# First feed-forward block by seven block products, with the squares of three of four quads on VectorE

## What is computed

```python
def rms_norm(x, w):
    y = xf * lax.rsqrt(jnp.mean(xf * xf, axis=-1, keepdims=True) + RMS_EPS)
    return (y * w)

def squared_relu_mlp(h, w_up, w_down):          # w_up 1024 x 4096, w_down 4096 x 1024
    return jnp.square(jax.nn.relu(h @ w_up)) @ w_down

x = x + y                                        # y: the mixer's output, through dn_out
x = x + squared_relu_mlp(rms_norm(x, norm_mlp), mlp_w_up, mlp_w_down)
```

## Time and profile before

| | before |
|---|---|
| median of 3 runs | 3104.36 us |
| profiled execution, its time | 3103.91 us |
| profiled execution, its span | 3102.1 us |
| mean granted TensorE clock | 0.987 |
| TensorE busy | 2953.6 us (95%), 14715 matmuls |
| VectorE busy | 1820.8 us (59%) |
| ScalarE busy | 1210.9 us (39%) |
| GpSimd busy | 901.7 us (29%) |

### The profile page before, as it was taken

The page is one execution under the profiler, slowest core; times in us unless marked ns, Lnnn a source line. Parts: engine busy times, 40 slices in busy tenths (PEclk is TensorE's granted clock), DMA queues, the critical chain, the costliest instruction groups (busy, mean ns, idle before and its releaser), DMA issues.

```text
span 3102.1 us, 37785 instructions
## 1 busy us (share of the span) xinstructions
PE 2953.6 (95%) x14715; PEld 2445.9 (79%) x14715; DVE 1820.8 (59%) x2359; ACT 1210.9 (39%) x1929; POOL 901.7 (29%) x684
## 2 busy tenths in 40 slices
PE   7899999989999999999998999999989999999997
PEld 6688888878788888888876777888878778887886
DVE  7566566564365544333366886554574866666866
ACT  5555555553311112221334776222332444444222
POOL 5333332221000000000302886331331444443423
PEclk9999999999999999999999999999999999999999
DMA  3111111112143333111210001011023144446953
GB/s 128 41 48 48 48 48 48 42 62 102 41 129 110 111 113 102 48 48 54 93 53 21 11 9 49 28 35 35 21 75 149 40 157 150 148 148 239 371 207 122
DMA packets 96833, 274.00 MB, mean 88 GB/s; under 512 B 9232, under 2 KB 31248, under 8 KB 92176
## 3 DMA queue, kind: packets, MB, share of 16 engines
q1 hardware_dynamic: 96656, 271.58, 25.0%
HBM read 208.43 MB, written 60.36 MB: 87 GB/s over the span
## 4 chain that ended last, share of the span: by engine, by line
PE 81%; DVE 10%; ACT 4%; issue 3%; POOL 1%; DMA 1%; SPq 0%; POOLq 0%; DVEq 0%; ACTq 0%
PE ps L663 25%; PE ps L1756 11%; PE ps L3068 11%; PE ps L3729 9%; PE ps L3096 7%; DVE b L3677 2%; PE ps L2659 2%; PE ps L1060 1%; DVE b L652 1%; PE ps L2466 1%; PE ps L2437 1%; PE ps L2465 1%; PE ps L1067 1%; PE ps L2480 1%; PE ps L90 1%
## 5 line engine op out<-in xcount | busy, mean ns | idle before, releaser
L663 PE MATMUL ps<-b 128*128 128x512 f32 x3912 | 1009.6, 403 | 29.7 <-DVE b L652 14.4
L663 PEld LDWEIGHTS ps<-b 128*128 128x128 f32 x3912 | 711.4, 191 | 159.2 <-issue 20.1
L1756 PE MATMUL ps<-b 128*128 128x512 f32 x1536 | 361.7, 396 | 0.6 <-DVE b L1924 0.6
L1756 PEld LDWEIGHTS ps<-b 128*128 128x128 f32 x1536 | 288.0, 188 | 69.5 <-DVE b L1924 1.0
L3729 PE MATMUL ps<-b 128*128 128x512 f32 (+1 forms) x1464 | 326.1, 377 | 6.3 <-ACT b L3788 5.9
L3729 PEld LDWEIGHTS ps<-b 128*128 128x128 f32 x1464 | 253.8, 191 | 55.6 <-issue 10.6
L644 ACT ACTIVATE b<-b 128x1024 fp32r<-128x1024 f32 x138 | 145.2, 1054 | 319.5 <-PE ps L1756 242.3
L3121 ACT ACTIVATE b<-b 128x512 fp32r<-128x512 f32 x232 | 142.3, 615 | 270.9 <-PE ps L3096 106.3
L652 DVE TENSOR_TENSOR b<-b 128x1024 fp32r<-128x1024 f32 x138 | 174.2, 1264 | 107.6 <-ACT b L644 98.5
L3068 PE MATMUL ps<-b 128*128 128x512 f32 x960 | 225.9, 393 | 6.0 <-DVE b L3371 3.8
L3068 PEld LDWEIGHTS ps<-b 128*128 128x128 f32 x960 | 180.5, 189 | 48.3 <-DVE b L3371 7.7
(11 more groups left out here) (372 smaller groups left out, 5011.4 us busy)
## 6 DMA issues: line engine op xcount, KB each, us to landing
inner<-b SPq DMA_DIRECT2D x77, 512.0 KB, 2.6
b<-inner SPq DMA_DIRECT2D x35, 1024.0 KB, 13.5
b<-in_down SPq DMA_DIRECT2D x52, 512.0 KB, 4.3
b<-in_mod SPq DMA_DIRECT2D x96, 256.0 KB, 2.6
b<-scratch SPq DMA_DIRECT2D x46, 512.0 KB, 4.4
b<-in_gu SPq DMA_DIRECT2D x44, 512.0 KB, 4.1
b<-in_dn_in SPq DMA_DIRECT2D x32, 512.0 KB, 4.9
b<-in_up SPq DMA_DIRECT2D x32, 512.0 KB, 3.7
```

The costliest lines, as they stand in the source:

```text
L663: ins = e.matmul(ps[:, c], w, h[:, k, c], start=first and k == 0 and i == 0, stop=last and k == KT - 1 and i == 2)
L1756: ins = e.matmul(ps[:, c], w, u[:, at[k], c], start=k == 0 and p == 0, stop=k == n - 1 and p == 2)
```

## The change

The first feed-forward block gets the same scheme. In words:

- 16 up blocks of two FF tiles each. Block 0 is plain (96 matmuls); blocks 1 to 15 have 7 steps of 12. Then 16 down blocks with 7 steps of 12 each. The last two up blocks are interleaved.
- The norm's factor is no longer applied to each up tile: since relu and square let a positive factor per token pass as its square, the block's result is scaled once, at the end, by 1/(mean of squares + eps), and added to x1, which was kept in DRAM meanwhile (`dve_square_last`, in the steps of the last down block: per half tile one multiplication with a row in PSUM, then one addition to x1, each waiting for the one before).
- Per up block VectorE joins three quads with a bank and squares them in place, max(u, 0) * u in one operation; the fourth quad ("21"), and all four of block 0, get relu and square as two ScalarE operations. GpSimd makes four sums of weight quads and four of inner quads. Seven pieces per block are split and stored to DRAM; the down blocks load them back (two blocks' pieces at a time, ring of 9).
- The modulation's slots: 12 of its steps now lie beside dn_out, then one every third up step, one every second down step.
- The statistics of the next norm (`act_stat2`, `pool_stat2`) use the rows of the scaled result as buffers, so their first square waits until x1 rows 0 to 3 are done.
- `PIECES7`, the order of pieces, is changed in the second block too.

The core of the diff:

```diff
+BLOCKS1 = tuple(((2 * b, 2 * b + 1),) for b in range(8))
+PIECES7 = (0, 3, 5, 4, 1, 2, 6)
...
+class WideSquare(Wide):
+    def sums(self, s):
+        if s == self.index[self.na, 0] + 13:
+            return self.na - 1
+        if s == self.index[0, 3] + 4:
+            return 0
+        v = self.which(s - 1, "last")
+        return v if v is not None and 0 < v < self.na - 1 else None
+    def beside(self, s):
+        a, b = self.index[self.na - 2, 0], self.index[self.na, 0]
+        return 6 <= s < a and s % 3 == 0 or s >= b and s % 2 == 0
...
+    def dve_square(self, e, w):
...
+        for i in range(KT):
+            if i:
+                self.dve_weights(e, min(jd + i + 3, jd + KT))
+            for _ in range(2 if i >= 2 else 0):
+                next(beside)
+            if 3 <= i < 7:
+                plain(i - 3)
+            if i == KT - 1:
+                for s in range(4):
+                    self.dve_wide_low(e, w, s)
+                for k in range(4, 7):
+                    plain(k)
+            x = self.x1[:, i, :]
+            e.wait_ge(*self.xl[i].at("dn_out"))
+            e.wait_ge(*self.gm.at(jd + i))
+            e.tensor_tensor(x, x, self.psl[i % 3], ALU.add).then_inc(*V.up("add", i))
...
+        for s in range(4, len(w.steps)):
+            v, i = w.steps[s]
...
+                if 3 <= i < 6:
+                    name = ("12", "22", "11")[i - 3]
+                    u = w.quads(v)[name]
+                    e.wait_ge(*P.at("st", v, i))
...
+                    e.tensor_tensor(u, u, self.square_bank(v, (1, 0, 2)[i - 3]), ALU.add).then_inc(*V.up("q" + name, v))
+                    e.wait_ge(*V.last())
+                    e.scalar_tensor_tensor(out=u, in0=u, scalar=0.0, in1=u, op0=ALU.max, op1=ALU.mult).then_inc(*V.up("u" + name, v))
+            else:
+                self.dve_square_add(e, w, v - w.na, i)
+            self.dve_wide_low(e, w, s + 6)
+            piece = w.piece(s)
+            if piece:
...
+                e.wait_ge(*A.at("thi", p, n))
+                e.tensor_tensor(b[:, 512:1024], w.source(p, PIECES7[n]), b[:, 0:512].bitcast(F32),
+                                ALU.subtract).then_inc(*V.up("tlo", p, n))
+            if v == last:
+                for k, f in {0: ((0, 0), (0, 1)), 1: ((1, 0), (1, 1)), 2: ((2, 0), (2, 1)), 3: ((3, 0), (3, 1), (4, 1), (6, 1)),
+                             4: ((5, 1), (7, 1)), 5: ((4, 0), (6, 0)), 6: ((5, 0), (7, 0))}[i]:
+                    self.dve_square_last(e, w, k, f)
+            if w.beside(s):
+                next(beside, None)
...
+        self.dve_weights(e, w.j0 + 2)
+    def dve_square_last(self, e, w, k, f):
...
+        e.wait_ge(*P.at("rw"))
+        e.wait_ge(*V.last())
+        e.tensor_tensor(y, y, self.psl[3][:, c], ALU.mult).then_inc(*V.up("scaled", k, f))
+        e.wait_ge(*self.xl[k].at("x1"))
+        e.wait_ge(*V.last())
+        ins = e.tensor_tensor(x, x, y, ALU.add)
...
+    def act_square(self, e, w):
...
+            if v == last:
+                for k in {2: (0, 1), 3: (2, 3)}.get(i, ()):
+                    e.wait_ge(*V.at("x1", k))
+                    if k == 0:
+                        e.wait_ge(*V.at("x1", 3))
+                        e.wait_ge(*A.at("cw"))
+                    self.act_stat2(e, self.m1, w.sig, k)
...
+        for k in range(4, KT):
+            e.wait_ge(*V.at("x1", k))
+            self.act_stat2(e, self.m1, w.sig, k)
+        self.act_weights(e, w.j0 + 2)
...
+    def pool_square(self, e, w):
...
+        for s in range(4, len(w.steps)):
...
+            self.pool_wide_sums(e, w, s, 1)
+            p = w.sums(s)
+            if p is not None:
+                u, tq = w.quads(p), w.tq
+                if p:
+                    e.wait_ge(*V.at("tlo", p - 1, 6))
...
+                e.tensor_tensor(tq[0], u["12"], u["11"], ALU.subtract).then_inc(*G.up("t", p, 1))
+                e.wait_ge(*G.last())
+                e.tensor_tensor(u["12"], u["22"], u["12"], ALU.subtract).then_inc(*G.up("t", p, 4))
+                e.tensor_tensor(tq[1], u["22"], tq[0], ALU.subtract).then_inc(*G.up("t", p, 2))
+                e.wait_ge(*G.last())
+                e.tensor_tensor(tq[2], u["21"], tq[1], ALU.subtract).then_inc(*G.up("t", p, 6))
...
@@ sp_between
-            e.wait_ge(*self.mm1[2].at("down", last, k))
+            e.wait_ge(*self.mm1[2].at("x1", k))
```

More of the change, by code:

```diff
@@ L348, in __init__ @@
         n = n_ff
-        self.steps = [(v, i) for v in range(2) for i in range(4)] + [(v, i) for v in range(2, n - 2) for i in range(7)]
+        self.steps = [(v, i) for v in range(n - 2) for i in range(self.last(v) + 1)]
         self.steps += [(n - 2, 0)]
@@ L368, in last @@
     def last(self, v):
-        return 3 if v < 2 else 6
+        return 3 if v < self.plain else 6
     def which(self, s, i):
@@ L641, in act_weights @@
             e.wait_ge(*self.wl[j % RAW].at(j))
-            if j >= SPL:
+            after = j - UNIT["win", 4]
+            if 0 <= after < SPL:
+                steps = self.w1.steps
+                e.wait_ge(*self.mm1[0].at("st", *steps[max(s for s in range(len(steps)) if s // 2 % SPL == after)]))
+            elif j >= SPL:
                 e.wait_ge(*self.gm.at(j - SPL))
@@ L1640, in mlp_slots @@
-    def mlp_slots(self, n_ff, ring, gated):
-        slots = []
-        for kind, f, n in mlp_plan(n_ff, ring):
-            if kind == "up":
-                slots.append((1, ("act", f)))
-                if gated:
-                    slots.append((2, ("mul", f)))
-            else:
-                slots += [(2, ("down", f, m)) for m in range(8)]
-        if not gated:
-            slots = [(2, ("relu", event[1])) if event[0] == "act" else (engine, event) for engine, event in slots]
-        return slots
@@ L3546, in pool_program @@
         self.pool_delta(e)
[L3547 to L3553 removed]
+        self.pool_square(e, self.w1)
         self.pool_stat2(e, self.m1, self.mm1)
```

942 lines of the change are left out of this document (502 added, 440 removed).

## The result

The changed kernel took 3160.22 us (median of 4 runs, 3158.26 to 3161.66); the kernel before, beside it, 3103.76 us. The ratio is 1.0182 (95% interval 1.0164 to 1.0199): **slower by 1.8%**, where 3091.5 was forecast and 3124 was the upper end of the range. The profiled execution took 3158.26 us, span 3156.4, mean granted clock 0.970 (0.987 before). TensorE is busy 2899.0 us instead of 2953.6, so most of the matmul time did go (84 us were forecast). VectorE is busy 2154.0 instead of 1820.8, GpSimd 1209.5 instead of 901.7.

What follows compares the result with a forecast made beforehand. It took TensorE's matmuls to bound the kernel before, VectorE the new up blocks. Terms -83.9 -9.9 +1.0 +5.5 +2 +36 -8 +4 +37.7 +3 sum to -12.6 us: from 3103.91 to 3091.3, stated as 3091.5, range 3062 to 3124.

Steps and rivals of the forecast that it cites:

- Matmuls (-83.9): Whole first feed-forward stage: matmul time falls from 707.0 us to 623.1 us, a gain of 83.9 us.
- The end (+37.7): Stage end: waiting for VectorE's x1 and GpSimd's sums, 48.1 us beyond matmuls before the projection, against 10.4: 37.7 more.
- E: End of the last down block's first product; the first projection was forecast at E + 64.7 us.
- The up blocks (22.5 us, measured 25.0): Blocks 2 to 13: VectorE, colliding with GpSimd, sets 22.5 us a block against TensorE's 19.5, adding 36 us in all.
- held by every GpSimd operation: Rival for the up blocks: every GpSimd operation blocks VectorE, 24.9 us a block, 3120 us in all; chance 0.22.
- ceiling of 25.8: Up blocks: VectorE's 16.6 us alone a block, plus all eight GpSimd operations holding it, give 25.8 us.
- the modulation's matmuls would be hidden (-8): Up blocks: while VectorE sets the pace, some 8 us of TensorE's modulation matmuls cost nothing extra.
- The modulation's slots: Beside dn_out: VectorE about 4 us late, 1.5 for slow matmuls; down steps: VectorE under 2.8 us per step, nothing added.
- The list of what would be wrong: Signs against the forecast: up blocks of 19.5 us, mid-stage TensorE waits for DMA, start after dn_out over 10 us late.
- transfers were taken as nothing (253 GB/s against 245): Up blocks: 253 GB/s was near the 245 of the second block's down steps, where TensorE never idled; no cost.
- Opening and block 1 (+5.5 and +2): Start of the stage: late VectorE 4 us plus slow matmuls 1.5; block 1's operands from GpSimd late, 2 us.
- counting it as two SBUF inputs: VectorE's in-place square in up blocks contends with GpSimd; counted as one input, the estimate falls 1.8 us a block.

Runs made afterwards that it cites:

- experiment 6: Changed kernel with x1's weighted squares summed by TensorE instead of GpSimd and projection weights loaded ahead of x1's stores: 3160.02 us, ratio 1.0182.
- experiment 14: experiment 13 plus early squares and sums of the next norm in buffers of their own, weights loaded earlier, x1 operations paired: 3091.17 us, ratio 0.9962.
- experiment 2: Changed kernel with VectorE's squares given back to ScalarE as relu and square, two operations: 3164.66 us.
- experiment 1: Changed kernel with no modulation slots beside the up blocks, the remaining ones at two of three down steps: 3210.39 us, ratio 1.0346.
- experiment 3: Changed kernel with GpSimd's four inner sums 8 columns wide instead of 512, values not the reference's: 3118.48 us, ratio 1.0049.
- experiment 5: Changed kernel with VectorE's modulation multiply-adds 8 columns wide instead of 512, slots and loads kept, values not the reference's: 3118.39 us, ratio 1.0050.
- experiment 10: Changed kernel with the edits of experiment 3, experiment 5 and experiment 7 together: 3069.18 us, ratio 0.9891.
- experiment 7: Changed kernel with four buffers for the modulation's loads instead of two, loads issued one slot earlier: 3140.27 us, ratio 1.0120.
- experiment 9: Changed kernel with all 16 up blocks plain, four modulation load buffers, modulation slots at two of three up steps: 3092.51 us, ratio 0.9962.
- experiment 11: experiment 9 with two more modulation slots in the up steps: 3101.01 us, ratio 0.9989.
- experiment 13: experiment 11 with the context rows read six slots later: 3092.54 us, ratio 0.9971.

## Why the prediction was wrong

**Matmuls (-83.9): right.** Where nothing else is late, the 168 matmuls of two up blocks took 38.60 us and 938 matmuls of the down steps 213.67, 0.230 and 0.228 each, if anything under the forecast's 0.232 and 0.230.

**The end (+37.7): right in size**, 62.1 us against 64.7, and GpSimd's adds do follow one another there, from E + 21.5 to E + 52.0, where the forecast had 22.2 and 52.0. Its mechanism was told too simply: were GpSimd's chain the only limit, experiments 6 and 14 would have gained 8 us or more. With early sums VectorE's additions to x1 took longer (experiment 14), and either one sets about the same end.

**The up blocks (22.5 us, measured 25.0): the step that failed is the 22.5 itself, which took VectorE's busy time for the block's time.** The busy time came out right: 272.13 / 12 = 22.7 us a block. Part of that is luck: the sum had 4.6 modulation operations at 0.748 us, which counts tiles of which some take two operations and prices them in a stage where GpSimd was nearly idle; it was 5.2 at 1.10, 5.7 us instead of 3.4. The splits and pieces took 13.4 us instead of 11.5. Added up by mean durations, as the forecast did it, the operations make 24.1 us instead of 20.2 + 2.3; since the records overlap a little, the busy time is 22.7. VectorE also stood still for 2.3 us a block, and the forecast had no term for that: mostly on ScalarE's high parts (22.5 us over the twelve), which waited for GpSimd's sums of weights, which waited for VectorE's low parts. Experiment 2 agrees, with the reserve made there: 40 us less work on VectorE came back as waits. Experiments 1, 3, 5 and 10 took work off VectorE or GpSimd and left the ring as it was, and the blocks fell. The rival "held by every GpSimd operation" named 24.9 us a block and was right in size; its reason (busy time near the ceiling of 25.8) was not what happened, and its 3120 leaves 38 us that lie outside these blocks. That TensorE cannot run ahead, and that the modulation's matmuls would be hidden (-8), belongs to the same step: they stood at the head of TensorE's queue and waited.

**The modulation's slots (nothing in the down steps; beside dn_out 4 us and 1.5, for VectorE's arithmetic alone): the second failure: +19.4 us in the down steps, +11.9 beside dn_out and in the opening.** The forecast's "under 2.8 us" of VectorE per step, with nothing added, counted arithmetic and left out that VectorE waits for each load in order; beside dn_out and in the opening it stood 16.2 us on these loads. Experiments 7 (-20 us, 13 of them in the down steps) and 5 (down blocks still 29 to 30 us) show the loads as a cause; experiment 1 shows the price when all of them lie there. The list of what would be wrong had "TensorE waiting for DMA"; it was VectorE that waited for DMA, and TensorE for VectorE. That transfers were taken as nothing (253 GB/s against 245) compared throughput, while what mattered was the time from issue to landing (7.0 to 11.5 us) of a load that could be issued only two ahead.

**Opening and block 1 (+5.5 and +2): too small by 13.5 us in block 1, 2.8 before it.** TensorE waited 7.0 us there with the modulation's matmul at the head of its queue, for VectorE's mean of squares behind the low parts; experiment 7 got 11 us back up to the end of block 1, 7 of them beside dn_out, and none in block 1. Without the modulation's slots (experiment 1) block 1 took 27.9 us, so 7 of its 13.5 us belong to them. How the rest splits between late operands and the low granted clock (0.85) was not taken apart.

**VectorE's square as one operation: worth 4.4 us at most** where nothing was forecast. On counting it as two SBUF inputs, the forecast was right: 0.910 us on average, 0.827 with 40% of GpSimd's work away, 0.69 for single ones clear of GpSimd's operations and 1.07 for the one above.

The Trainium skill says in the section used for the up blocks (SBUF — State Buffer, "Who interferes with whom") that a VectorE copy or tensor_scalar can take the shared port pair too, through its two-port mode. The trace agrees: L2212, a tensor_scalar with one SBUF input, took 909 ns in these blocks against 479 for the same operation before, in a stage where GpSimd was nearly idle.

## What to carry to other kernels

When three in-order engines feed each other, the busiest one's time is a floor, not the forecast: add the waits of the ring, or test which engine's relief shortens it. In a chain of waits, read a load as the time from issue to landing, and take the idle time of an engine from its own timeline: the two differed here (11.5 us against 6.3 in the down steps, 14 against 3.3 at the passage of experiment 9). A side job that is free beside one stage is not free beside another, even with its arithmetic hidden: count how far ahead its loads can be issued, and who is queued behind its waits. And fewer matmuls can be bought too dear: with the same load buffers, seven products in the down half only, where pieces come ready from DRAM, beat seven in both by 48 us (3092.5 against 3140.3), with the side job's slots placed to suit.

## What the runs showed that was not expected

- The granted clock mostly followed the waits: 1.00 in all stretches where TensorE was never idle, 0.94 in the up blocks, 0.85 in block 1, 0.88 and 0.65 in the two parts of the end, where 12 matmuls after a wait of 6.1 us took 5.46 us instead of 2.8. But the passage of experiment 14 had 4.4 us of waits in 28 us at 1.00.
- Matmuls of plain blocks ran at 0.231 us inside the dense stretch of experiment 9, against 0.227 per matmul in the plain products of the kernel before.
- The chain of waits at the passage named another cause in each run (modulation group in 9, context row in 11, piece store in 13), while TensorE stood 3.3, 10.1 and 3.9 us and the transfers there ran at 366 to 387 GB/s.
